# The second feed-forward of a two-block model: a new order of the activation casts around the weight casts

## The reference, cut to what matters

```python
h = rms_norm(x, norm_mlp)                       # 1024 x 1024
x = x + jnp.square(jax.nn.relu(h @ w_up)) @ w_down   # w_up 1024 x 4096, w_down 4096 x 1024
return rms_norm(x, norm_final)
```

## Time and profile before

| | |
|---|---|
| median of 3 runs | 2858.85 us (2854.32 to 2860.6) |
| the profiled execution | 2861.63 us, its span 2859.9 us |
| PE busy | 2724.5 us (95%) |
| DVE, ACT, POOL busy | 1750.1, 1129.4, 1754.1 us |
| granted TensorE clock, mean | 0.982 of full speed |
| this stage | from 2157.4 us to the end; its loop begins each round 42.66 us after the last on average |

### The profile page before, as it was taken

One profiled execution on the slowest core, in us unless ns is written; L12 is line 12 of the kernel. 1 busy time (PEld: TensorE's weight loads), 2 busy tenths in 40 slices (PEclk: granted clock), 3 DMA queues, 4 the chain that ended last, 5 costly groups with the idle time before them and its releaser, 6 DMA issues. The chain is left out here.

```text
span 2859.9 us, 39241 instructions
## 1 busy us (share of the span) xinstructions
PE 2724.5 (95%) x13371; PEld 2246.3 (79%) x13371; DVE 1750.1 (61%) x2209; ACT 1129.4 (39%) x1684; POOL 1754.1 (61%) x1201
## 2 busy tenths in 40 slices
PE   8999998999999999799999999999998999999998
PEld 7888886888888887678778878878786777777776
DVE  5334435565555656575685685685535877777778
ACT  4312316333332334555355345445333433443443
POOL 3323336767777676765565565565337787777782
PEclk9999999999999999899999999999999999999999
DMA  3111111111212113212111111112601111111112
GB/s 121 45 38 37 45 38 30 45 44 51 59 46 64 44 51 96 66 34 60 49 49 60 49 48 59 49 48 59 221 15 44 45 44 59 44 44 59 44 47 92
DMA packets 196117, 160.28 MB, mean 56 GB/s; under 512 B 5719, under 2 KB 176300, under 8 KB 196013
## 3 DMA queue, kind: packets, MB, share of 16 engines
q1 hardware_dynamic: 196013, 158.83, 18.1%
HBM read 143.08 MB, written 15.73 MB: 56 GB/s over the span
## 5 line engine op out<-in xcount | busy, mean ns | idle before, releaser
L340 POOL TENSOR_TENSOR w_lo<-w_raw,w_hi 128x512 fp32r<-128x512 f32 x336 | 466.2, 1395 | 316.9 <-ACT w_hi L334 316.9
L334 ACT CAST w_hi<-w_raw 128x512 fp32r<-128x512 f32 x336 | 202.8, 617 | 432.3 <-DMA w_raw<-in_w_in 106.2
L546 PE MATMUL PA<-h_hi,w_hi 128*128 128x512 f32 x636 | 260.7, 410 | 17.7 <-PEq L1035 5.6
L548 PE MATMUL PA<-h_hi,w_lo 128*128 128x512 f32 x636 | 250.0, 393 | 0.0
L547 PE MATMUL PA<-h_lo,w_hi 128*128 128x512 f32 x636 | 249.7, 393 | 0.0
L340 POOL TENSOR_TENSOR w_lo<-f_sums,w_hi 128x512 fp32r<-128x512 f32 x128 | 201.8, 1577 | 10.5 <-ACT w_hi L334 10.5
L396 POOL TENSOR_TENSOR w_raw<-w_raw,params 128x1024 f32<-128x1024 f32 x72 | 137.2, 1918 | 90.1 <-DMA w_raw<-in_w_up 45.5
L340 POOL TENSOR_TENSOR w_lo<-hy_ring_sums,w_hi 128x512 fp32r<-128x512 f32 x96 | 140.4, 1463 | 61.6 <-ACT w_hi L334 61.6
L546 PE MATMUL PB<-f_t_hi,w_hi 128*128 128x512 f32 x424 | 169.4, 400 | 8.5 <-ACT hy_tm L2797 5.0
L547 PE MATMUL PB<-f_t_lo,w_hi 128*128 128x512 f32 x424 | 166.3, 392 | 0.0
L548 PE MATMUL PB<-f_t_hi,w_lo 128*128 128x512 f32 x424 | 166.3, 392 | 0.0
(11 more groups left out here) (664 smaller groups left out, 8273.2 us busy)
## 6 DMA issues: line engine op xcount, KB each, us to landing
w_raw<-in_w_in SPq DMA_DIRECT2D x64, 512.0 KB, 5.2
w_raw<-in_ffn_w_up SPq DMA_DIRECT2D x42, 512.0 KB, 4.7
w_raw<-in_w_down SPq DMA_DIRECT2D x32, 512.0 KB, 3.7
w_raw<-in_w_up SPq DMA_DIRECT2D x30, 512.0 KB, 4.7
w_raw<-in_gla_w_in SPq DMA_DIRECT2D x24, 512.0 KB, 3.7
w_lo_raw<-in_ffn_w_down SPq DMA_DIRECT2D x44, 256.0 KB, 2.6
X<-in_x SPq DMA_DIRECT2D x8, 512.0 KB, 7.8
w_raw<-in_gla_w_out SPq DMA_DIRECT2D x8, 512.0 KB, 3.6
```

The costliest lines, as they stand in the source:

```text
L334: act.copy(self.slot(i, p)[0], source).then_inc(self.hi_done, 1)
L340: pool.tensor_tensor(lo, source, hi.bitcast(F32), ALU.subtract).then_inc(self.split, 1)
L546: pe.matmul(bank, ah[:, k, :], bh[:, k, :], start=(k == 0 and not more), stop=False, skip_group_check=more)
L548: mm = pe.matmul(bank, al[:, k, :], bh[:, k, :], start=False, stop=(k == 3), skip_group_check=more)
```

## The change

In `rise`, ACT casts the activation blocks P1 and P4 ahead of the seventh up weight, then the first two down weights, then P5, then runs `keep`, then casts P2 (A12) and the other five down weights. `MADE` follows that order, DVE makes the low part of P2 after its third sum, and `keep` waits for the low part of P5 as number 3. In `fall`, the casts of P6, P7 and P3 and `relu_first` stand together ahead of the next chunk's first weight cast, and `relu_second` ahead of its second. Ahead of the loop, the same order is written out for chunks 0 and 1, the two differences on `X` follow `combine(0)` instead of standing first, and the second raw tiles lie over the places of P2/P7 and P5/P3 instead of P1/P6 and P2/P7, with the waits that follow from it.

```diff
-        MADE = ("P1", "P2", "P4", "P5", "P6", "P7", "P3")
+        MADE = ("P1", "P4", "P5", "P2", "P6", "P7", "P3")
...
-            ring.give_second([self.at(f"{name}_second_raw{k}", [P, UNIT], base + at * UNIT) for k, at in enumerate((8, 12))],
+            ring.give_second([self.at(f"{name}_second_raw{k}", [P, UNIT], base + at * UNIT) for k, at in enumerate((12, 22))],
...
-                        act.wait_ge(s["a_lo"], made(i, 4))
+                        act.wait_ge(s["a_lo"], made(i, 3))
...
-                            else:
-                                act.wait_ge(ring.split, ring.done(1, 5))
+                            elif x == "P2":
+                                act.wait_ge(ring.split, ring.done(1, 4))
...
                 def rise(i):
 
+                    a_high(i, "P1", "P4")
                     high(i, 6)
-                    a_high(i, "P1", "P2", "P4", "P5")
+                    for n in range(2):
+                        ring.row_high(act, i, n)
+                    a_high(i, "P5")
                     keep(i)
-                    for n in range(7):
+                    a_high(i, "P2")
+                    for n in range(2, 7):
                         ring.row_high(act, i, n)
 
                 def fall(i, following):
 
-                    a_high(i, "P6")
+                    a_high(i, "P6", "P7", "P3")
+                    relu_first(i)
                     following(0)
-                    a_high(i, "P7")
-                    relu_first(i)
-                    a_high(i, "P3")
-                    following(1)
                     relu_second(i)
-                    for n in range(2, 6):
+                    for n in range(1, 6):
                         following(n)
...
-                dve.tensor_tensor(X12, X12, X22, ALU.subtract)
-                dve.tensor_tensor(X21, X21, X22, ALU.subtract)
...
-                    for x in ("P1", "P2", "P4"):
+                    for x in ("P1", "P4"):
                         a_low(i, x)
                     dve.tensor_tensor(A22, A21, A22, ALU.add).then_inc(s["a_sum"], 1)
                     dve.tensor_tensor(A21, A11, A21, ALU.subtract).then_inc(s["a_sum"], 1)
                     a_low(i, "P5")
                     dve.tensor_tensor(A11, A22, A11, ALU.subtract).then_inc(s["a_sum"], 1)
+                    a_low(i, "P2")
...
                 combine(0)
+                dve.tensor_tensor(X12, X12, X22, ALU.subtract)
+                dve.tensor_tensor(X21, X21, X22, ALU.subtract)
```

More of the change, by code:

```diff
@@ L2163, in a_high @@
                                 act.wait_ge(ring.used, ring.done(i - 1, 13))
+                            else:
+                                act.wait_ge(ring.split, ring.done(1, 5))
                         act.copy(ahi[PLACE[x]], BLOCK[x]).then_inc(s["a_hi"], 1)
@@ L2192, in _ @@
                 high(0, 6)
-                high(1, 0, 1, 2, 3, 4)
+                high(1, 0, 1, 2)
                 relu_first(0)
+                high(1, 3)
                 relu_second(0)
-                high(1, 5)
+                high(1, 4, 5)
                 rise(1)
```

## The result

The changed kernel takes 2923.43 us (median, 2922.86 to 2926.41) against 2858.95 us of the kernel before: 1.023 times, 95% interval 1.0213 to 1.0248. The profiled execution spans 2921.7 us against 2859.9 us, 61.8 us more.

A forecast was written before the change was run, and what follows sets the result against it. It took the chain of waits through POOL, idle 3.90 us a round, as the bound. Start -1 us, 13 rounds of +3.3 us and end +2.7 us, added to the 2858.85 us median, gave 2903 us; range 2870 to 2918 us.

The forecast's parts named there:

- the loop: New chain of waits through all engines, once a round: 45.9 us, bounds 41.8 to 46.6, against 42.66 before.
- a: POOL's low part of up P2 starts, to the down rows being there: 5.4 us taken.
- b: On ACT, two down weight casts waiting for their loads, until P5's cast starts: 2.1 us taken.
- c: P5's cast, its low part and the third sum on DVE, until `keep` starts: 4.0 us taken.
- e: PE's product P2 at the low clock after its wait: 5.0 us taken, bounds 3.3 to 5.0.
- f: PE's five products up P4 and P3, down P1, P2 and P5: 13.6 us.
- g: From PE's start of the product after down P5 to `relu_first`: 2.4 us taken, bounds 1.8 to 2.4.
- i: POOL's low part of up P1 to that of P2: 10.1 us taken, second weight cast behind `relu_second`.
- Ahead of the loop: Start of the stage, up to POOL's P2 of round 2: -1 us.
- Behind the loop: From L510 of round 15 to the first addition of the last product: +2.7 us.
- My rival with PE at full clock: P2 alone at 3.3 us: round 44.2 us, time 2881 us; chance 0.14 shared with the case of DVE not held.
- The rival of the other side: POOL's own loop sets the pace, `keep` in time: round 38.8 us, 2803 us; all faster cases 0.11.

The follow-up runs named there:

- e4_one_row_ahead: Changed kernel with the second of the two down weight casts moved behind `keep`, the first still ahead of P5: 2903.38 us.
- e6_pe_kept_busy: Changed kernel with 20 more matmuls, read by nothing, on PE each round ahead of its wait for `keep`: 2913.3 us.
- e3_rows_behind_keep: Changed kernel with the first two down weight casts moved behind `keep` and the cast of P2: 2848.46 us.
- the four runs behind it: Changed kernel with four activation casts ahead of `keep` and all down weight casts behind it, in four variants of order and `fall`: 2828.8 to 2832.45 us.
- e10_p4_first_weight_early: e7_four_casts_p4_first with the seventh up weight cast ahead of `keep` and the next chunk's first weight cast ahead of `relu_first`: 2828.8 us.
- e7_four_casts_p4_first: Changed kernel with casts P4, P1, P5, P2 ahead of `keep`, seventh up weight and all down weights behind; changed `fall` kept: 2831.14 us.
- e8_four_casts_weight_early: Changed kernel with P1, P4, P5, P2, seventh up weight cast ahead of `keep`, down weights behind; next chunk's first weight ahead of `relu_first`: 2830.34 us.
- e1_old_fall: Changed kernel with the old order of `fall` put back, the new `rise` kept: 2875.46 us.

## Where the prediction was right, and the step that failed

The direction, the loop and its signs were as forecast: two casts waiting for `w_down`, PE waiting 5.3 to 5.7 us ahead of P2 with the clock at 0.50 behind it, 3.3 us of POOL's idle time ahead of up P1, no wait of 2.64 us in the down product. The loads are 47.07 us apart, 1 us more than the 45 to 46 us of the sign. The time was 20 us above mine and 5 us outside the range. The steps, in the round shown above and in the mean of the 13 rounds from POOL's P2 of round 2 to that of round 15:

| step | taken (bounds), us | this round, us | from | mean, us |
|---|---|---|---|---|
| a, POOL's P2 to the rows | 5.4 (5.0 to 5.5) | 5.48 | 2659.12 - 2653.64 | 5.52 |
| b, two casts to P5 | 2.1 (1.8 to 2.2) | **3.28** | 2662.40 - 2659.12 | **3.03** |
| c, P5 to `keep` | 4.0 (3.2 to 4.25) | 3.76 | 2666.16 - 2662.40 | 3.76 |
| d, `keep` to P2 | 0.64 | 0.72 | 2666.88 - 2666.16 | 0.71 |
| e, f, g, P2 to `relu_first` | 21.0 | 21.09 | 2687.97 - 2666.88 | 21.40 |
| h, to POOL's P1 | 2.7 | 2.71 | 2690.68 - 2687.97 | 2.71 |
| i, P1 to P2 | 10.1 (9.8 to 10.3) | 9.94 | 2700.62 - 2690.68 | 9.94 |
| sum | 45.94 | 46.98 | | 47.08 |

**The step that failed is b**, "Two down weight casts, then the cast of P5 starts. The second load follows one POOL instruction later (1.3 us, or 1.7 if stretched), and a cast adds 0.5." I took the second load to be as long as the first. The stretch to 1.7 us was there (3.44 us for the two low parts), but the second load also took longer. The first low part ends near 2653.64 + 1.72 = 2655.4 us and its tile is there at 2659.1 us, 3.7 us later; the second ends at 2657.08 us and its tile is there at 2661.88 us, 4.8 us later. Over the 13 rounds b takes 2.74 to 3.32 us, where I had at most 2.2 us: 0.93 us more than I took. With a, 0.12 us more, this is 1.05 us of the 47.08 - 45.94 = 1.14 us by which the mean round missed my sum. The other steps nearly cancel: e, f and g together took 0.40 us more, about what PE waited for DVE's takes in the down product (5.6 us in 13 rounds); c took 0.24 us less and i 0.16 us less. The 1.14 us make 14.8 us over 13 rounds.

e4_one_row_ahead shows that the second load lies on the loop: without it ahead of P5, step b is 0.53 us and the round 1.3 us shorter. It does not measure the excess of b. Not the whole of b goes there, since the second load then holds what stands behind `keep`, and P2 to `relu_first` takes 23.2 us in the mean.

That the second load is the longer one stood in the trace of the kernel before, where nothing waited for it. There the tiles of the down rows land 1.4 to 2.2 us one after the other, 1.8 us in the mean, for releases 1.26 us apart; in the changed kernel they land 2.2 to 2.8 us apart, 2.5 us in the mean, for releases 1.7 us apart. The two loads of round 2 in the kernel before, from issue to landing:

```profile
DMA to landing us min/median/max: 3.6/4.0/4.3
```

The rows of the two ends, POOL's P2 of rounds 2 and 15 and L510 of round 15, then DVE's first addition of the last product:

```profile
2229.49 3.43 POOL L340 TENSOR_TENSOR w_lo<-w_raw,w_hi 128x512 fp32r<-128x512 f32 x2
...
2841.54 3.44 POOL L340 TENSOR_TENSOR w_lo<-w_raw,w_hi 128x512 fp32r<-128x512 f32 x2
...
2846.92 1.29 POOL L510 TENSOR_TENSOR f_sums<-w_raw 128x512 f32<-128x512 f32 x1 [0.25 <-DMA w_raw<-in_w_down]
```

```profile
2891.69 0.69 DVE L2294 TENSOR_TENSOR X<-X,DD 128x512 f32<-128x512 f32 x1
```

**The rest of the 20 us.** *Ahead of the loop* I took -1 us, and POOL's P2 of round 2 is at 2229.49 against 2230.40 us: -0.9 us. *Behind the loop* I took +2.7 us. From L510 of round 15 to the first addition of the last product it was +3.6 us (44.77 against 41.17 us), 0.9 us more than I had, by b again (2.99 us in that round), and from POOL's P2 to the end of the span +5.0 us (80.16 against 75.14 us, where P2's low part of round 15 was at 2784.76 us), of which 1.1 us are the last product, whose first matmuls ran at the low clock for longer: +2.3 us more than I had. And I had set the gain of 44 us on the median of the runs, 2.8 us under the profiled execution; the changed kernel's profiled execution lies on its median, so 2.7 us of the difference are this choice. 14.8 + 2.3 + 2.7 = 19.8 us.

**Step c and the Trainium skill.** The row at 2663.05 us shows the low part at 1.34 us and the row at 2664.31 us the sum at 1.74 us, and the two low parts of POOL's P2 and P4 took 3.44 us where they took 2.55 to 2.57 us in the kernel before. The Trainium skill ("SBUF — State Buffer", Who interferes with whom) says that a VectorE instruction with two SBUF inputs contends with a GpSimd instruction that reads SBUF; the trace agrees with it in direction. By the prediction's estimate of the worst case of that rule c would have been 4.5 us, and it was 3.76 us. POOL's rows beside the two instructions of DVE show why:

```profile
2662.57 1.27 POOL L340 TENSOR_TENSOR w_lo<-w_raw,w_hi 128x512 fp32r<-128x512 f32 x1 [0.95 <-ACT w_hi L334]
2663.80 1.71 POOL L515 TENSOR_TENSOR w_raw<-w_raw 128x512 f32<-128x512 f32 x1
```

POOL's two instructions end at 2663.84 and 2665.51 us, and DVE's two at 2664.39 and 2666.05 us, 0.55 us behind each. They were late by what was left of POOL's instruction, 0.65 and 1.05 us more than 0.69 us, and not by all of it.

**Step e came near by accident.** 5.0 us was taken for a whole product at the low clock, and the mean was 4.97 us. But it varies from 4.26 to 5.28 us with the moment at which the clock comes back, some 3 to 6 us behind the start of P2, and the lower bound of 3.3 us was wrong: e6_pe_kept_busy has the full clock and 4.28 us, since a sum on DVE takes 1.80 us there and not 0.69 us. My rival with PE at full clock (2881 us) would have been 2913 us.

**The rival of the other side.** That POOL's loop could set the pace if `keep` came in time was right as a mechanism: e3_rows_behind_keep and the four runs behind it are that case. Its size was not. I had 38.8 us a round and 2803 us; the four last runs are at 40.46 to 40.89 us and 2829 to 2832 us. The 38.8 us kept POOL's instructions as long as they were; in e10_p4_first_weight_early they are longer by 1.8 us a round, which makes 40.6 us. That this is all of it is not shown: in e7_four_casts_p4_first POOL is hardly busier than before (433.78 against 429.55 us over 13 rounds), and waits for the seventh up weight cast behind `keep` instead, 3.0 us a round.

## What to carry to other kernels

A cast or a copy that another engine waits for must not stand, on an in-order engine, behind an instruction that waits for a load, unless that load was released by something far ahead of it; here two casts of 0.5 us put in front of `keep` cost 75 us. What made them so dear was the second half of the loop: with the old `fall` the same order is only 15 us behind the kernel before. Before an order is changed, close the loops: follow the wait from engine to engine until it comes back to where it began, add the times up, and compare with the present round. In such a sum count each of two loads released one after the other by its own landing, not by the first one's and the distance of the releases.

## What the runs showed of the hardware

- Two loads of 512 KB released 1.7 us apart in the same queue: in the rounds of the changed kernel the user of the first starts 3.6 to 4.0 us behind the release, that of the second 4.4 to 4.8 us (2657.08 to 2661.88 us in the round shown). The second takes 4.5 to 4.9 us in e7_four_casts_p4_first and in e8_four_casts_weight_early. Whether the queue, the transfer or the memory makes the difference, no run here tells.
- What PE waited, and what followed: behind 2.25 us in e1_old_fall the matmuls were at the full clock's pace at once. Behind the 2.64 us in the kernel before the granted clock was 0.59 over 3.49 us. Behind 3.11 us ahead of the last product it was 0.61 over 4.41 us in the kernel before, and behind 3.08 us at the same place 0.50 over 4.75 us in the changed kernel, whose PE had also waited 5.28 us some 33 us earlier. No run here takes the two waits apart. The window of the last one:

```profile
2887.25:2892.00 4.75, 4.75 (x11) 3.78 (x12) 4.66 (x3) 0.00 (x0) 0.00 (x0) 0.50 0.00 0
```

- The low clock behind a wait of over 5 us costs less than it looks, where another engine must be waited for next: 0.73 us a round here, although the 12 matmuls of P2 took 2.15 us longer in the round shown.
